# Output projection of the mixer in four PSUM banks, begun before the last prompt head is done, with the sample attention among its tiles

## What is computed

```python
def mixer_ab(hn, attend, conv_buf, h0, w_in, w_out, ...):
    q, k, v, qi, ki, wi, g, xr = split_cols(hn @ w_in, AB_SPLITS)
    attn = attend(q, k, v, qi, ki, wi)            # 8 heads; prompt: 128 of up to 512 keys a query
    rg, new_buf, h_last = rglru_branch(g, xr, conv_buf, h0, ...)
    return jnp.concatenate([attn, rg], axis=-1) @ w_out, ...

def sample_sparse_attention(q, k_new, v_new, qi, ki_new, wi, ck, cv, cik, page_table, rel_bias):
    _, idx = lax.top_k(where(admissible, indexer_scores(qi, wi, ki_all), -inf), 256)   # of 4097
    k_sel, v_sel = ...                            # gathered from the paged cache, or the new row
    return gathered_attention(q, k_sel, v_sel, ...)

yp = yp + out                                     # residual; then RMSNorm and the feed-forward stage
```

## Time and profile before

| | us |
|---|---|
| median of 3 runs (lowest, highest) | 1331.13 (1331.06, 1331.21) |
| the profiled execution, its own time | 1329.75 |
| its span | 1328.0 |
| TensorE busy | 1264.8 (95%) |
| VectorE busy | 699.2 (53%) |
| ScalarE busy | 466.3 (35%) |
| GpSimd busy | 191.8 (14%) |

### The profile page before, as it was taken

The page is one execution under the profiler, slowest core; times in us unless marked ns, Lnnn a source line. Parts: engine busy times, 40 slices in busy tenths (PEclk is TensorE's granted clock), DMA queues, the critical chain, the costliest instruction groups (busy, mean ns, idle before and its releaser), DMA issues.

```text
span 1328.0 us, 24456 instructions
## 1 busy us (share of the span) xinstructions
PE 1264.8 (95%) x9998; PEld 1220.0 (92%) x10001; DVE 699.2 (53%) x1279; ACT 466.3 (35%) x540; POOL 191.8 (14%) x285
## 2 busy tenths in 40 slices
PE   6999998978999999999999999989999999999995
PEld 5979995757989999999999999989999999999994
DVE  5478996474456555555323255534655555542223
ACT  5242326533234343433222244332443434331110
POOL 1001101117031111111000010041311111110000
PEclk9999997685999999999999999999999999999997
DMA  6664311001313222222222332122222222222211
GB/s 218 167 119 155 104 31 41 1 21 46 115 51 126 79 83 90 95 95 95 88 88 87 102 127 93 64 80 79 96 81 81 91 95 95 95 87 88 87 61 64
DMA packets 26016, 118.25 MB, mean 89 GB/s; under 512 B 7816, under 2 KB 9160, under 8 KB 13928
## 3 DMA queue, kind: packets, MB, share of 16 engines
q1 hardware_dynamic: 21208, 105.58, 24.1%
q0 software_dynamic: 2048, 10.54, 2.4%
q10 hardware_dynamic: 2704, 1.35, 0.4%
HBM read 113.85 MB, written 3.61 MB: 88 GB/s over the span
## 4 chain that ended last, share of the span: by engine, by line
PE 88%; DVE 7%; POOL 2%; issue 1%; ACT 1%; DMA 1%; DVEq 0%; SPq 0%; ACTq 0%
PE ps L818 22%; PE ps L819 22%; PE ps L821 22%; PE ps L949 4%; PE ps L952 3%; PE ps L950 3%; PE ps L898 2%; PE ps L999 1%; PE ps L1020 1%; POOL xl L1817 1%; PE ps L835 1%; DVE xc L1382 1%; PE ps L882 1%; PE ps L863 1%; PE ps L1010 1%
## 5 line engine op out<-in xcount | busy, mean ns | idle before, releaser
L818 PE MATMUL ps<-xh,w_h 128*128 128x260 f32 x1792 | 471.2, 284 | 9.2 <-POOL xl L1817 9.1
L819 PE MATMUL ps<-xl,w_h 128*128 128x260 f32 x1792 | 469.3, 283 | 0.0
L821 PE MATMUL ps<-xh,w_l 128*128 128x260 f32 x1792 | 361.1, 283 | 0.0
L818 PEld LDWEIGHTS ps<-xh,w_h 128*128 128x128 f32 x1792 | 339.3, 189 | 10.6 <-issue 7.6
L819 PEld LDWEIGHTS ps<-xl,w_h 128*128 128x128 f32 x1792 | 338.8, 189 | 0.1
L1240 DVE TENSOR_TENSOR w_l<-w_raw,w_h 128x2048 fp32r<-128x2048 f32 (+1 forms) x94 | 211.6, 2251 | 162.6 <-ACT w_h L503 162.4
L821 PEld LDWEIGHTS ps<-xh,w_l 128*128 128x128 f32 x1792 | 276.9, 189 | 0.0
L503 ACT ACTIVATE w_h<-w_raw 128x2048 fp32r<-128x2048 f32 (+1 forms) x50 | 92.3, 1846 | 278.5 <-PE ps L821 243.1
L819 PE MATMUL ps<-hl,w_h 128*128 128x260 f32 x704 | 184.0, 283 | 0.0
L818 PE MATMUL ps<-hh,w_h 128*128 128x260 f32 x704 | 183.6, 283 | 0.0
L821 PE MATMUL ps<-hh,w_l 128*128 128x260 f32 x704 | 141.9, 283 | 0.0
(11 more groups left out here) (297 smaller groups left out, 1419.7 us busy)
## 6 DMA issues: line engine op xcount, KB each, us to landing
w_raw<-in_wstream SPq DMA_DIRECT2D x86, 1024.0 KB, 4.7
w_raw<-in_wstream SPq DMA_DIRECT2D x8, 768.0 KB, 4.3
res<-in_x_t SPq DMA_DIRECT2D x4, 520.0 KB, 7.0
out_y<-yt SPq DMA_DIRECT2D x8, 260.0 KB, 2.2
tab<-bias_by_distance SPq DMA_DIRECT2D x16, 128.0 KB
wm<-in_sgu_w ACTq DMA_DIRECT2D x1, 512.0 KB, 3.8
sb_b<-in_sgu_b ACTq DMA_DIRECT2D x1, 512.0 KB, 4.3
out_f<-ost SPq DMA_DIRECT2D x2, 198.0 KB, 4.5
```

The lines of the kernel that those rows point to most:

```text
L818: pe.matmul(out[h], wh, hi[h], start=(first and k == 0), stop=False)
L819: pe.matmul(out[h], wh, lo[h], start=False, stop=False)
L821: ins = pe.matmul(out[h], wl, hi[h], start=False, stop=(last and k == nk - 1))
```

## The change

The kernel after the change is the same program up to the last slab of the input projection, but for the placement of small tiles in memory. What it does from there:

- **PE.** `out_stage("out_ab")` is gone. `out_tiles(g)` does slab 10+g as two halves t (one output tile each) of 8 steps k, all in banks 0 to 3. A half waits until DVE has added the same half of the slab before. It begins right after `p_work(32)`. After each step `beside_out(g, step)` puts in one piece of the work that stood ahead: tie counts, the last head, the 16 placing products, the last block's turn, key turns, logits, weights and values of the samples. The first slab takes its steps with k from 0 to 3 first. Sample attention moves to banks 4, 5, 6 and 7.
- **Late rows.** The attention columns of the 8 samples are zero in `xh` and `xl` during the projection. `sample_rows` adds them: 32 products of 8 columns in plain fp32, with the attention half of the weights loaded again (`wor`, 4 transfers of 512 KB), and one DVE addition to `res`.
- **DVE.** `split` of slab 10 moves ahead of the bisection, that of slab 11 into round 13, and the scans into rounds 21 to 25. The rest of its program is one list, written out, with halves added (`add_half`), placing rows, splits and squares in turn. It fills `xl` tiles 4 to 7 itself (`attention_low`).
- **ACT.** `split` of slab 10 and of slab 11 come before the rounds. `xh` tiles 0 to 3 are filled in rounds 29 to 32.
- **POOL.** The gathers stand behind the recurrence's product and the `xl` tiles 0 to 3.
- **Warm products.** Three a round in rounds 0 to 8, two a round in rounds 9 to 13.
- **SP.** Slab 12 loads early; the four `wor` transfers and slab 13 wait for the last head's logits, slab 15 for the late rows.

The diff, cut to its core:

```diff
-            sp.wait_ge(w_hi, 10)
-            sp.wait_ge(w_lo, 10)
-            load(11, 1)
+            for t in (11, 12):
+                sp.wait_ge(w_hi, t - 1)
+                sp.wait_ge(w_lo, t - 1)
+                load(t, t % 2)
             sp.wait_ge(hst_done, 1)
             sp.dma_start(h_o, hst[:]).then_inc(d_out, 16)
             sp.dma_start(c_o, cst[:]).then_inc(d_out, 16)
-            sp.wait_ge(x_lo, 16)
+            sp.wait_ge(qpad_done, 1)
+            sp.wait_ge(lg_done, 32)
+            for g in range(4):
+                sp.dma_start(wor[:, g], wstream[10 + g, :, 4 * 256:].rearrange("p (k c) -> p k c", c=256)).then_inc(d_wor, 16)
+            for t in (13, 14):
+                sp.wait_ge(w_hi, t - 1)
+                sp.wait_ge(w_lo, t - 1)
+                load(t, t % 2)
+            sp.wait_ge(late_done, 1)
             sp.dma_start(st[:], ffn0[0]).then_inc(d_st, 16)
+            sp.wait_ge(w_hi, 14)
+            sp.wait_ge(w_lo, 14)
+            load(15, 1)
 
             def load_loop(first, n):
 
@@ -475,7 +491,7 @@
...
+            act.wait_ge(slab_done, 10)
+            split(11, 1)
...
+                if 29 <= rnd < 33:
+                    fill_high(1, rnd - 29, gg[:, rnd - 29, :], rg_done, rnd - 28)
...
-            out_stage("out_ab", 1, FILL["up0"])
+            split_next(10)
+            act.wait_ge(x_lo, 12)
+            group_squares("out_ab", 1, 0)
+            keys_turned(0)
+            hot_turned()
+            keys_turned(1)
+            split_next(11)
+            group_squares("out_ab", 1, 1)
+            sample_exp(0)
+            keys_turned(2)
+            keys_turned(3)
+            weights_turned(0)
+            split_next(12)
+            sample_exp(1)
+            group_squares("out_ab", 1, 2)
+            weights_turned(1)
+            act.wait_ge(slab_done, S0["out_ab"] + 4)
+            fill_scaled(1, FILL["up0"], (0, 1))
+            group_squares("out_ab", 1, 3)
+            fill_scaled(1, FILL["up0"], range(2, KT_D))
+            split_next(13)
+            norm_root(1)
...
+            split(10, 0)
...
+                if rnd == 13:
+                    dve.wait_ge(e_done, 4)
+                    dve.memset(atr[:, :, SEQ:T], 0.0)
+                    split(11, 1)
+                if 21 <= rnd < 25:
+                    rg_scan(rnd - 21)
+                if rnd == 25:
+                    rg_samples()
...
+            def attention_low(j):
+
+                dve.wait_ge(at_ev, NCH)
+                dve.wait_ge(x_lo, 12)
+                dve.wait_ge(x_hi, 13 + j)
+                tt(xl[:, 4 + j, :], atr[:, j, :], xh[:, 4 + j, :].bitcast(F32), ALU.subtract).then_inc(x_lo, 1)
+
...
+            def sample_rows():
+
+                p64 = lambda a: a.rearrange("p (b h) -> p b h", h=8)
+                dve.wait_ge(pv_mm, 1)
+                ch.link(tt(o1[:], p64(ps[:, 4, 0:64]),
+                           vt[:, SEQ:T].rearrange("p (b a) -> p b a", a=1).broadcast_to((P, DEC, 8)), ALU.mult))
+                ch.link(tt(o1[:], o1[:], p64(ps[:, 4, 64:128]), ALU.add))
+                for h in range(2):
+                    ins = dve.tensor_copy(at64[64 * h:64 * h + 64], o1[64 * h:64 * h + 64, :, 4 * h:4 * h + 4]
+                                          .rearrange("p b j -> p j b"))
+                ins.then_inc(at64_done, 1)
+                dve.wait_ge(late_mm, 1)
+                dve.wait_ge(a_free, G0["out_ab"] + 3)
+                tt(res[:, :, SEQ:T], ps[:, 4, P:P + 64].rearrange("p (k b) -> p k b", b=DEC), res[:, :, SEQ:T], ALU.add)\
+                    .then_inc(late_done, 1)
+                dve.wait_ge(late_done, 1)
...
+            for i in range(3):
+                slot_row(i)
+            for j in range(4):
+                attention_low(j)
+            for i in range(3, 11):
+                slot_row(i)
+            add_half(0, 0)
+            add_half(0, 1)
+            for i in range(11, 16):
+                slot_row(i)
+            hot_buckets()
+            split_next(10)
+            add_half(1, 0)
+            add_half(1, 1)
+            sample_least(0)
+            split_next(11)
+            add_squares(1, 1, a_free, 12)
+            sample_weights(0)
+            add_half(2, 0)
+            add_half(2, 1)
+            sample_least(1)
+            sample_weights(1)
+            split_next(12)
+            add_squares(1, 2, a_free, 13)
+            sample_rows()
+            dve.wait_ge(x_lo, 16)
+            dve.wait_ge(b_free, 13)
+            scaled(1, FILL["up0"], ("norm_ffn", 0), (0, 1, 2))
+            sample_squares()
+            add_half(3, 0)
+            add_half(3, 1)
+            dve.wait_ge(b_free, 14)
+            scaled(1, FILL["up0"], ("norm_ffn", 0), (3,))
+            add_squares(1, 3, a_free, 14)
+            scaled(1, FILL["up0"], ("norm_ffn", 0), range(4, KT_D))
+            split_next(13)
+            norm_scale(1)
...
-            for q in range(4):
-                pool.wait_ge(rows2_done, q + 1)
-                for s4 in range(4):
-                    i = 4 * q + s4
-                    pool.indirect_dma_start(out=kv[:, q, s4, :], out_offset=None, in_=cache_kv,
-                                            in_offset=bass.IndirectOffsetOnAxis(ap=row2[:, i:i + 1], axis=0)).then_inc(kv_in[q], 16)
...
-
-                for n in range(3):
-                    pe.matmul(ps[:, 3, :], sameb[:], pickb[NCH - 1][:], start=True, stop=True)
+            def warm(k):
+
+                for n in range(k):
+                    pe.matmul(ps[:, 6, :], sameb[:], pickb[NCH - 1][:], start=True, stop=True)
 
             pe.wait_ge(topk_done, 3)
             for rnd in range(32):
                 count(rnd)
-                if rnd < 8:
-                    warm()
+                if rnd < 9:
+                    warm(3)
                 p_work(rnd)
-
-            pe.wait_ge(sel_cnt, 1)
-            pe.matmul(tied, sameb[:], cntb[:, 2:3], start=True, stop=False)
-            pe.matmul(tied, beforeb[:], cntb[:, 3:4], start=False, stop=True).then_inc(tie_mm, 1)
-            p_work(32)
-            pe.wait_ge(sel_cnt, 2)
-            pe.matmul(before_me, beforeb[:], cntb[:, 4:5], start=True, stop=True).then_inc(base_mm, 1)
-            for rnd in range(33, NROUNDS):
-                p_work(rnd)
-
-            pe.wait_ge(in_row, 2)
-            for i in range(16):
+                if 9 <= rnd < 14:
+                    warm(2)
+
+            def tie_counts():
+
...
+            def slot_ranks(i):
...
-                if i < 3:
-                    pe.wait_ge(lg_done, 32)
-                else:
+                if i == 0:
+                    pe.wait_ge(in_row, 2)
+                    pe.wait_ge(pt_ev, 32)
+                if i >= 3:
                     pe.wait_ge(g_free, i - 2)
-                pe.matmul(ps[:, i % 3, 0:NP], inrow2[s % 2][rows_, h * P:(h + 1) * P], ptab[rows_, :], start=True,
+                pe.matmul(ps[:, (4, 5, 7)[i % 3], 0:NP], inrow2[s % 2][rows_, h * P:(h + 1) * P], ptab[rows_, :], start=True,
                           stop=True).then_inc(g_mm, 1)
-            p_out(NCH - 1)
-            pe.wait_ge(hot_done, 1)
-            pe.wait_ge(at_ev, NCH)
-            for q in range(4):
-                ins = pe.transpose(ps[:, 6, q * P:(q + 1) * P], hot_b[:, 4 * q:4 * q + 4, :].rearrange("p s j -> p (s j)"),
-                                   ident[:])
-            ins.then_inc(hot_mm, 1)
...
+            def beside_out(g, step):
+
+                n = 16 * g + step
+                if n == 1:
+                    tie_counts()
+                if n == 2:
+                    p_work(33)
+                if n == 4:
+                    chosen_before()
+                if n == 5:
+                    p_work(34)
+                if n == 7:
+                    for i in range(3):
+                        slot_ranks(i)
+                    p_out(NCH - 1)
+                if 8 <= n < 21:
+                    slot_ranks(n - 5)
+                if n == 24:
+                    keys_turn(0)
+                if n == 25:
+                    hot_turn()
+                if n == 29:
+                    keys_turn(1)
+                if n == 31:
+                    sample_logits(0)
+                if n == 37:
+                    keys_turn(2)
+                if n == 44:
+                    keys_turn(3)
+                if n == 45:
+                    weights_turn(0)
+                if n == 46:
+                    sample_logits(1)
+                if n == 47:
+                    sample_values(0)
+                if n == 51:
+                    weights_turn(1)
+                if n == 53:
+                    sample_values(1)
+                if n == 56:
+                    sample_rows()
+
+            def out_tiles(g):
+
+                s, slot = S0["out_ab"] + g, g % 2
+                pe.wait_ge(w_lo, s + 1)
+                order = [(t, k) for t in range(2) for k in range(8)]
+                if g == 0:
```

(35 more changed lines are left out.)

202 lines of the change are left out of this document (98 added, 104 removed).

## The result

The changed kernel took 1319.81 us (median of 4 runs, 1317.3 to 1322.03) against 1331.11 for the kernel before: a ratio of 0.9914, interval 0.9897 to 0.9932. The forecast was 1318.0. The runs of the kernel before lay within 0.2 us in that comparison, those of the changed one within 5. Run again on other chips, it came to 0.9904 (0.9890 to 0.9918) and 0.9935 (0.9915 to 0.9954). The profiled execution was the quickest of the four, 1317.3 us of its own time and a span of 1315.6, 12.4 under the one of before.

What follows compares the result with a forecast made beforehand. TensorE (PE) was taken to bound the kernel, busy 95%, partly at half clock. Terms -19.2 - 0.8 + 3.4 + 1.8 + 1.7 = -13.1 from 1329.75 gave 1316.65, plus 1.38 for the median: 1318.0 us; range about 1305 to 1327.

Steps and rivals of the forecast that it cites:

- The clock in rounds 9 to 16: Rounds 9 to 13: -0.8 us; round 13's split idles PE about 2.4, clock falls, rounds 14 to 16 cost as before.
- rival A: Clock survives round 13, rounds 14 to 16 run at 2.4 GHz: a further -6.7 us, 1311.3; chance 0.25.
- Rounds 17 to 20: Square roots on ACT, 1.94 us, costed at nothing because ACT is idle for over half of these stretches.
- The scans: Scans moved into rounds 21 to 25 on DVE: +3.4 us, bounds 0 and +4.9.
- POOL beside DVE: Rounds 25 to 32, recurrence's product and `xl` fills slow DVE's one-column steps: +1.8 us, bounds 0 and 4.6.
- Rival C: Every POOL instruction in rounds 25 to 32 blocks DVE for 0.58 us: +4.6 for +1.5, 1321.1; chance 0.12.
- The projection: Last head's logits to projection's end: 79.0 us against 98.2, -19.2, including 5.7 of stalls; clock falls counted apart.
- at one chance in three for each: Clock falls at two short PE waits, first attention tile and slab 11, 2.5 us each: +1.7, between 0 and +5.0.
- The gathers: On POOL's queue behind product and fills, landing before step 24: costed at nothing, up to 1.3 us if late.
- D: DVE runs late in the projection, both gaps drop the clock and stand twice as long: 1323.3 us; chance 0.13.
- E: Slower: clock stays at half from round 8 until slab 11: +5.3 us, 1336.4; chance 0.04.
- F: Gathers land late, sample attention stands behind the projection with nothing beside it: 1333.5 us; chance 0.03.

Runs made afterwards that it cites:

- e2: Kernel before with only the added warm products (three in round 8, two a round in rounds 9 to 13): 1323.78 us, ratio 0.9944.
- e3: Changed kernel without the added warm products, three a round in rounds 0 to 7 as before: 1325.77 us, ratio 0.9955.
- e9: Changed kernel with POOL's gathers of keys and values held until slab 10 is done: 1325.28 us, ratio 0.9980.
- e4: Changed kernel with DVE's add of slab 10's first half moved ahead of placing rows 8 to 10: 1316.59 us, ratio 0.9888.
- e5: Changed kernel with the 32 late products spread, four behind each of steps 54 to 61: 1318.41 us, ratio 0.9925.
- e7: Changed kernel with twelve warm products in round 19 and six before the first attention tile: 1316.02 us, ratio 0.9902.
- e10: Changed kernel with the edits of e4, e5 and e7 together: 1319.91 us, ratio 0.9936.
- e12: e10 with 14 more warm products in the last slab, behind the samples' values and the late products: 1309.98 us, ratio 0.9877.
- e11: Changed kernel unedited, run again for the third group of runs: 1318.98 us, ratio 0.9935.
- e8: Changed kernel with placing products 4 to 15 two at a time behind every other step: 1319.35 us, ratio 0.9917.
- e1: Changed kernel unedited, run again for the first group of runs: 1317.32 us, ratio 0.9904.

## Why the forecast held though its terms did not

- **The clock in rounds 9 to 16.** Rounds 9 to 13 went as forecast. The step that failed is "So PE idles for about 2.4 us just there, and I expect the clock to fall after it". PE's wait in round 13 was 0.80 us, since for most of the split (225.93 to 228.18) it still had the heads of round 12, the warm products, the count and the first pair of round 13 to do, and it was 0.73 in round 15. The clock stayed at 1.00. That is rival A, given 0.25, and it came at its price: -5.7 for -6.7. e2 and e3 show it from both sides.
- **Rounds 17 to 20** were costed at nothing, with 1.94 us for the square roots. ACT is held for 4.5, since a table load stands on either side of them, as in the kernel before:

```profile
242.00 1.28 ACT L635 ACT_TABLE_LOAD   x1
243.29 1.94 ACT L635 ACTIVATE th<-th 128x2080 f32<-128x2080 f32 x1
245.25 1.28 ACT L643 ACT_TABLE_LOAD   x1
```

  At full clock PE ran ahead of ACT and then stood 3.35 us behind them (1.29 before), after which the clock fell. A net -1.0.
- **The scans** cost 1.6, not 3.4, within their bounds. The first (DVE, 250.42) hid under PE's round 20, which ran at half clock. Of the later rounds only 23 and 25 grew, by 1.26 and 0.33.
- **POOL beside DVE** cost 0.2, not 1.8. Rival C is wrong in its size, but its mechanism is in the rows. POOL's four instructions run from 245.31 and from 261.03, 1.25 us each:

```profile
245.31 5.01 POOL L2061 TENSOR_TENSOR ii<-ii,th 128x520 f32<-128x520 f32 x4 [31.35 <-ACT th L635]
...
261.03 5.03 POOL L2067 TENSOR_TENSOR gg<-gg,xc 128x520 f32<-128x520 f32 x4
```

```profile
245.90 0.70 DVE L1625 SCALAR_TENSOR_TENSOR sm<-sm 128x1 f32<-128x1 f32 x1
...
249.24 1.10 DVE L1625 SCALAR_TENSOR_TENSOR sm<-sm 128x1 f32<-128x1 f32 x1
...
261.94 0.39 DVE L1625 SCALAR_TENSOR_TENSOR sm<-sm 128x1 f32<-128x1 f32 x1
```

  DVE's one-column step ends at 246.60, 250.34 and 262.33. By their starts and equal lengths, POOL's first and fourth instruction of the first row and the first of the second end at 246.56, 250.32 and 262.29: this step waits for the rest of the instruction that it meets. That agrees with the rule of the Trainium skill (page "SBUF — State Buffer", section "Terms"), by which the loser of the shared port pair fully blocks for an instruction. The three steps are 1.7 us longer together, 0.55, 0.95 and 0.24, but only the last of them lies in rounds 25 to 31, where the forecast had seven steps and 1.5 us. It costs nothing where the round is PE's, and rounds 26 to 31 are as long as they were.
- **The projection** is the term that was mis-sized: -8.1 for -17.5. Of the 9.4 us, read from the spacing of PE's steps (0.72 us each at full clock, 1.13 with a placing product behind): the 13 placing products that stand alone cost 0.41 each, not 0.12, 3.8 in all; the samples' own work was 1.5 cheaper than its 15.5; the late products took 8.5 for 7.6, the last 3.0 us of it at half clock; the two waits 6.7, for 5.7 of stalls in all. The largest is "at one chance in three for each": the clock fell at both gaps, and a third time behind the late products, where no gap is. The eight steps at half clock cost 5.4 more in all, in place of 1.7. These make some 8 of the 9.4; the rest stays open.
- **The gathers** were costed at nothing because they would land in time. They did. What they cost is on PE while they are issued (e9, which shows that it goes with them, not by what path). The kernel before doesn't show it in its rows: PE was waiting for DVE there anyway.

The two large errors, the clock in rounds 14 to 16 and the projection, have opposite signs. The forecast is close because they cancel, together with the terms for scans and POOL, and nothing in the prediction foresaw that. Rivals D, E and F did not occur, though D's sign, waits in the projection with a falling clock, was that of the error.

## What to carry to other kernels

Where TensorE sits at half clock through a stretch that it bounds itself, try a few wide products ahead of it before any rebuilding: thirteen gave 7.65 us in the kernel before and 8.45 in the changed one. When work with few columns is moved in among full products, price it at its own duration and at the clock that it leaves behind; and if a wait is taken away, look for the next one before adding up gains (e4, e5, e7 and their sum e10 gave nothing clear of the spread; with the last fall closed as well, e12 is 8 us under e11).

## What was not expected of the hardware

- The clock fell, and stayed down, with PE busy the whole time: at 358 us behind 5.5 us of 8-column products, and in e10 for 20.5 us with PE busy for 20.17. With fourteen products of 512 columns among them it was at 1.00 (e12). It was so in e5's profile too, without them, so the late products do not make it fall each time. Rounds 14 to 16 ran the same work at 0.50 or at 1.00, as they were entered.
- Keeping falls away in one place doesn't leave the others as they were. In e7 those at 249 and 290 are gone, but the one in the last slab lasts 13.5 us, for 7 in the first profile. In e10 those from 244 to 346 are gone, and the last lasts 20.
- While POOL issues eight or more gathers in a row, DVE starts on a finished product up to 5 us after its record starts, in place of 0.3 to 0.5 (3.38 in the changed kernel, 3.95 in e9, 4.29 in e4, 5.36 in e8). That it moves with the gathers is shown by e9. By what path is open: no run tells it apart.
- The same wait of 1.27 us at 178 us was followed by a fall in some executions (the changed kernel's first profile, e4) and in others not (the kernel before, e1). That short waits widen the spread is not shown: the changed kernel's three groups of four to six runs span 4.7 to 8.1 us, the kernel before's later groups of 9 to 17 runs 3.4 to 7.2.
